# A two-layer decoder trunk on one core: modulation blocks moved out of the triangular solve into the feed-forward

## The reference, cut to what matters

```python
c_act = jax.nn.silu(c)
for l in range(DEPTH):
    mod = (c_act @ w_mod[l] + b_mod[l])[:, None, :]          # w_mod: (2, 1024, 6144)
    sh1, sc1, gt1, sh2, sc2, gt2 = jnp.split(mod, 6, axis=-1)
    h = rmsnorm(x, norm1_g[l]) * (1 + sc1) + sh1
    z = h @ w_cat                                            # one input projection
    ...                                                      # RG-LRU, differential attention, RWKV-7
    x = x + gt1 * (merged @ w_out[l])
    h2 = rmsnorm(x, norm2_g[l]) * (1 + sc2) + sh2
    x = x + gt2 * conv_gated_mlp(h2, ffn_up[l], ffn_conv_w[l], ffn_conv_b[l], ffn_down[l])
return rmsnorm(x, final_g)
```

## Time and profile before

| | |
|---|---|
| Median of 3 runs | 1259.96 us (1256.7 to 1268.15) |
| The profiled execution | 1261.44 us, of which its span 1259.6 us |
| PE busy | 1208.3 us, 96% of the span |
| DVE busy | 711.8 us, 57% |
| ACT busy | 446.4 us, 35% |
| POOL busy | 66.0 us, 5% |
| Mean granted TensorE clock | 0.989 of full speed |
| Moved from memory | 212.30 MB, 169 GB/s over the span |

### The profile page before, as it was taken

The page is one execution under the profiler, slowest core; times in us unless marked ns, Lnnn a source line. Parts: engine busy times, 40 slices in busy tenths (PEclk is TensorE's granted clock), DMA queues, the critical chain, the costliest instruction groups (busy, mean ns, idle before and its releaser), DMA issues.

```text
span 1259.6 us, 23676 instructions
## 1 busy us (share of the span) xinstructions
PE 1208.3 (96%) x10096; PEld 1098.7 (87%) x10096; DVE 711.8 (57%) x1108; ACT 446.4 (35%) x731; POOL 66.0 (5%) x108
## 2 busy tenths in 40 slices
PE   7999999989999999999999999999899999999997
PEld 6888888878788899999988788888787889999996
DVE  5465545255235689986435573525532557878643
ACT  2322234400123566664332130460012156666533
POOL 0010000011001000000000000000110200000000
PEclk8899999999999999999999999999999999999999
DMA  9755444154134456667535444333522444454530
GB/s 381 276 212 184 167 148 172 50 200 171 36 133 170 195 189 243 222 223 245 218 120 191 173 183 157 130 132 122 201 89 78 142 184 177 175 192 170 197 134 34
DMA packets 39332, 214.61 MB, mean 170 GB/s; under 512 B 6192, under 2 KB 6448, under 8 KB 19792
## 3 DMA queue, kind: packets, MB, share of 16 engines
q1 hardware_dynamic: 27728, 171.42, 37.4%
q0 software_dynamic: 11520, 41.95, 9.6%
HBM read 212.30 MB, written 1.05 MB: 169 GB/s over the span
## 4 chain that ended last, share of the span: by engine, by line
PE 90%; DMA 4%; DVE 3%; issue 1%; ACT 1%; SPq 0%; DVEq 0%; ACTq 0%
PE ps L1370 19%; PE ps L1357 12%; PE ps L1359 12%; PE ps L1358 12%; PE ps L1488 11%; PE ps L1689 7%; DMA mring<-wmod_dram 3%; PE ps L1574 3%; PE ps L1328 2%; PE ps L1335 1%; DVE macc L830 1%; PE ps L1319 1%; PE ps L1741 1%; DMA G<-wmod_dram 1%; PE ps L1565 1%
## 5 line engine op out<-in xcount | busy, mean ns | idle before, releaser
L1370 PE MATMUL ps<-H,ring 128*128 128x256 f32 x1088 | 241.7, 383 | 1.4 <-ACT H L487 1.4
L1370 PEld LDWEIGHTS ps<-H,ring 128*128 128x128 f32 x1088 | 208.1, 192 | 37.0 <-issue 9.0
L1224 DVE TENSOR_TENSOR WLO<-ring,WH 128x1024 fp32r<-128x1024 f32 x144 | 175.2, 1223 | 102.3 <-ACT WH L688 102.3
L688 ACT ACTIVATE WH<-ring 128x1024 fp32r<-128x1024 f32 x144 | 151.5, 1058 | 170.1 <-PE ps L1359 163.0
L1357 PE MATMUL ps<-HH,WH 128*128 128x256 f32 x736 | 208.3, 283 | 0.0
L1358 PE MATMUL ps<-HL,WH 128*128 128x256 f32 x736 | 208.3, 283 | 0.0
L1359 PE MATMUL ps<-HH,WLO 128*128 128x256 f32 x736 | 208.3, 283 | 0.0
L1488 PE MATMUL ps<-H,ring 128*128 128x256 f32 x768 | 179.1, 385 | 0.0
L1488 PEld LDWEIGHTS ps<-H,ring 128*128 128x128 f32 x768 | 141.7, 190 | 21.7 <-issue 1.6
L1357 PEld LDWEIGHTS ps<-HH,WH 128*128 128x128 f32 x736 | 141.3, 192 | 0.0
L1358 PEld LDWEIGHTS ps<-HL,WH 128*128 128x128 f32 x736 | 141.3, 192 | 0.0
(11 more groups left out here) (314 smaller groups left out, 1607.9 us busy)
## 6 DMA issues: line engine op xcount, KB each, us to landing
ring<-wmain_dram SPq DMA_DIRECT2D x150, 1024.0 KB, 4.8
mring<-wmod_dram POOLq DMA_DIRECT2D x80, 512.0 KB, 4.6
G<-wmod_dram SPq DMA_DIRECT2D x3, 1024.0 KB, 7.6
R<-wmod_dram SPq DMA_DIRECT2D x3, 1024.0 KB, 15.6
TK<-wmod_dram SPq DMA_DIRECT2D x2, 1024.0 KB, 21.4
C<-consts_dram SPq DMA_DIRECT2D x1, 1088.5 KB, 18.4
X<-x_t_dram SPq DMA_DIRECT2D x1, 1024.0 KB, 9.6
SW<-small_dram SPq DMA_DIRECT2D x2, 512.0 KB, 15.4
```

What stands on the lines that cost most here:

```text
L688: A(WH[:, n % 2, part], ring[:, b, part], ACT.Copy).then_inc(hi_ready, 1)
L1224: V.tensor_tensor(WLO[:, n % 2, part], ring[:, b, part], WH[:, n % 2, part].bitcast(F32), ALU.subtract).then_inc(lo_ready, 1)
L1370: last = MM(ps[:, g % 4, m * S:(m + 1) * S], w_of(g, m, i), rhs[:, i, :], start=(i == 0), stop=(i == KT - 1))
```

## The change

The solve keeps one modulation block behind each x and xt step in place of two, 8 in each layer in place of 16. So only vector 4 (10) is accumulated there, its sum takes the place in the merge where vector 5's (11's) stood, and PE's and DVE's places for a sum inside the solve are gone. Layer 0's vector 5 follows in the up stage; that pushes the later blocks back, and the down stage takes 14 blocks in place of 6: 2 in each of the first four pairs and 1 in each of the next six. Sums then stand behind down pairs 0 (vector 5), 3 (vector 6) and 10 (vector 7). Layer 1's vector 11 comes in its own down stage, which had no blocks: 1 in each of the first eight pairs, the sum behind pair 8. POOL issues layer-relative blocks up to 25 (two of them ahead) before the chunk chain and the rest after the merge's additions. DVE reads a sum one pair after PE's place for it.

```diff
-DN_BLOCKS = [1, 1, 1, 1, 1, 1, 0, 0, 0, 0, 0, 0]
-DN_SUM, DN_LAST = 1, 6
+DN_BLOCKS = [[2, 2, 2, 2, 1, 1, 1, 1, 1, 1, 0, 0], [1, 1, 1, 1, 1, 1, 1, 1, 0, 0, 0, 0]]
+DN_SUMS = [{0: 5, 3: 6, 10: 7}, {8: 11}]
...
-                mod_blocks(m0 + 18, m0 + 32)
+                mod_blocks(m0 + 18, m0 + 26)
...
-                if l == 0:
-                    mod_blocks(48, 66)
+                mod_blocks(m0 + 26, 66 if l == 0 else m0 + 32)
...
                         if par == 1 and v < 4:
-                            if (kind, v) == ("x", 2):
-                                mod_vector(6 * l + 4)
-                            mod_beside(2)
+                            mod_beside(1)
...
-                mod_vector(6 * l + 5)
+                mod_vector(6 * l + 4)
...
-                    if l == 0:
-                        if n == DN_SUM:
-                            mod_vector(6)
-                        if n == DN_LAST:
-                            mod_vector(7)
-                        mod_beside(DN_BLOCKS[n])
+                    if n - 1 in DN_SUMS[l]:
+                        mod_vector(DN_SUMS[l][n - 1])
+                    mod_beside(DN_BLOCKS[l][n])
...
-                        if (par, v) == (1, 2):
-                            pe.wait_ge(mod_ready, 6 * l + 5)
...
-                        if (kind, v) == ("x", 2):
-                            mod_sum(6 * l + 4)
...
-                mod_sum(6 * l + 5)
+                mod_sum(6 * l + 4)
...
                 for q in range(4):
                     down(0, q, True)
-                    if l == 0 and q == DN_SUM:
-                        mod_sum(6)
+                    if q in DN_SUMS[l]:
+                        mod_sum(DN_SUMS[l][q])
...
-                        if 4 + q == DN_LAST:
-                            mod_sum(7)
...
                 for q in range(4):
                     down(2, q, tail=True)
+                    if 8 + q in DN_SUMS[l]:
+                        mod_sum(DN_SUMS[l][8 + q])
                     if q >= 2:
                         ones_sum(2 * l + 2, (0, 6)[q - 2], (4, 8)[q - 2])
```

## The result

The changed kernel takes 0.9921 of the time of the kernel before, 95% interval 0.9902 to 0.994: medians of 20 runs each 1254.35 us (1248.34 to 1260.61) and 1263.95 us (1256.45 to 1271.97). That is 0.8% or 9.6 us faster; the interval leaves out 1, but the gain is under the 1% (12.6 us) that the prediction takes as the least change to be told from none.

What follows compares the result with a forecast made beforehand. PE, busy 96% of the span, was taken to bound the kernel; 1261.44 - 13.4 + 1.0 + 1.1 = 1250.1 us profiled, 1248.7 us for the median of runs, range 1245.5 to 1255.5.

Steps and rivals of the forecast that it cites:

- Part 1: Both solves: with one block per step, PE's waits for DVE's masks all go, a gain of 13.4 us.
- the 6 to 7 named as the sign: Sign for the solve: its window was to get shorter by 6 to 7 us in each layer.
- Part 2: One sum per layer moves from solve to down stage: -1.77 + 1.76 us, twice, is nothing.
- Part 3: Layer 0's down stage, two blocks per pair: PE waits 1.0 us for a transfer before vector 6's sum.
- 2T - 9.5: PE's wait in us before vector 6's sum, T being a block's landing time; nothing below T = 4.75.
- 4.9 to 7.8: Landing times in us expected in layer 0's down stage; landings outside them would show the prediction wrong.
- Part 4: Layer 0, vector 7's sum behind down pair 10: residual additions come late, PE waits 1.1 us for ACT's squares.
- Part 5: Layer 1's down stage: one block per pair in eight pairs, with the sum behind pair 8, costs nothing.
- (d): Rival, 0.04: transfers saturate in the down stage, PE waits 15.7 us at vector 6's sum; 1263.4 us, 1269 with lost clock.
- (a): Rival, 0.24: no transfer wait in the down stage, the solve gives its 13.4 us; -12.8 us, 1247.2 us.
- (b): Rival, 0.14: landings near 7.8 us move the transfer wait to the down stage, 6.1 us there; 1253.8 us.
- (c): Rival, 0.06: blocks still come late in the solve, half of the 13.4 us stays; -4.6 us, 1255.4 us.

Runs made afterwards that it cites:

- e4: The kernel before with every edit of the change made for layer 1 only, layer 0 left as it was; ratio 0.9926 to the kernel before.
- both edits: The changed kernel with vector 6's sum behind pair 4 and vector 7 read behind the residual additions; 0.9868 and, run again, 0.9862 of the kernel before.
- e6: The kernel before with 32 solve blocks read from constants already in SBUF, not transferred, so four vectors are wrong; 0.9842 of the kernel before, two runs.
- e1: The changed kernel with vector 6's sum behind down pair 4 in place of 3; 0.9875 of the kernel before.
- a0: The changed kernel again, nothing altered; 0.9906 of the kernel before, 7 runs.
- a1: The changed kernel again, nothing altered, run beside the kernel with both edits; 0.9929 of the kernel before, 12 runs.
- e2: The changed kernel with DVE reading vector 7 and forming the next norm's gain behind the residual additions of pairs 8 to 10; 0.991 of the kernel before.
- e3: The changed kernel with both edits, first time; 0.9868 of the kernel before, median 1247.02 us.
- e5: The changed kernel with unused matmuls keeping PE busy in layer 0's down stage, ahead of vector 6's sum and the squares' sum; 0.9888 of the kernel before.
- e8: The kernel with both edits run again beside the changed kernel; 0.9862 of the kernel before, median 1244.56 us.
- e7: The changed kernel with vector 6's sum behind down pair 2 in place of 3; one run, no ratio, PE waited 6.3 us before that sum.

## Why the prediction came out as it did

The forecast was 1248.7 us, 11.3 us or 0.9% less than its base; measured are 1254.35 us, 9.6 us or 0.8% less than the kernel before. Of the 5.7 us between forecast and result, 4.0 lie in the base and 1.7 in the gain. Direction and size were right. That the gain came so near was in part luck: in the profiled pair it is 5.0 us and not 11.3, because PE lost 6.3 us in layer 0's down stage that the sum doesn't have (5.2 of clock, 1.0 of wait at the first place, 0.1 at the second). The medians show 4.6 us more gain than the profiled pair, and no trace shows where, since the kernel before was profiled only once. The same holds for e4 (11.9 us by the medians, 7.3 by the stretch that it changes) and for both edits together (17.7 and 21.9 us by the medians, 14.0 and 13.1 from the first solve product on).

**Part 1** held in full. Waits for the masks in the solves went from 13.4 us to none (changed kernel), and e6 shows by itself that they were for the transfer and not for DVE's work. e4 shows layer 1's share by itself. The solve's stretch got shorter by 8.2 and 8.9 us and not by the 6 to 7 named as the sign: that sign left out the 1.8 us of the sum of part 2.

**Part 2** held: a sum costs 4.65 - 2.88 = 1.77 us in the down stage (e1), so the move is even.

**Part 3** had the right mechanism and place, and its term too small: 1.0 us against 2.0 in the first profile, 1.3, 1.6 and 3.5 in the three further runs that have the order and no filling. The formula 2T - 9.5 was 0.3 to 0.4 us low in all four, with the landings of each run put in; the rest is the landings. These were 3.9 to 6.7 us around a median of 5.2 (568 to 600) in the first profile and up to 7.9 in a0, so they left the 4.9 to 7.8 outside of which the prediction calls itself wrong; yet those that vector 6 waited for, 5.1 to 7.5 us, were inside. One landing of 7.5 us was enough for the 3.5 us of a1, and the T of the prediction was one number for all. e1 shows the cover that one pair more gives. That PE would never wait for `low` held too.

**Part 4** held: 1.2 us against 1.1, shown by e2.

**Part 5** held, shown by e4: no wait and no fallen clock.

**What failed** is that the sum has no term for the clock behind the waits of parts 3 and 4; rival (d) says of waits of about 1 us that they are shorter than those of the solve, which cost none. I had priced a fallen clock only for a wait of 15.7 us (rival d). The waits for the masks, up to 3.6 us, cost none in the two traces that have them (before and e4); waits of 1.2 to 2.0 us in the down stage of the first profile cost 1.8 and 3.4 us more. The missed term, 5.2 us, is larger than the two waits themselves, 3.2 us. So the length of a wait alone doesn't tell. Before or behind each wait of the down stage stands a sum, 1.8 us of one-column matmuls. The sum without a wait costs no clock (e1 and e3), and wait and sum together do, unless work fills the wait (e5). A sum that the change doesn't touch, in layer 0's input projection at about 90 us, says the same: in the nine profiled runs in which it follows without a wait there is no dip behind it, in the three in which PE stood 1.02, 0.53 and 0.37 us before it there is one. The shortest, in e8, and then PE's window behind it (busy, granted clock, DMA share, GB/s):

```profile
88.54 1.92 PE L1323 MATMUL ps<-sm,macc 128*128 128x1 f32 x16 [0.37 <-issue]
```

```profile
92.00:94.00 2.00, 2.00 (x6) 0.50 0.82 338
```

That is not the whole rule, though: the tail's wait and sum gave no dip in e1, and dips also follow waits without a sum (last section). What tells the cases apart is open, and a wait of the same length next to full matmuls in the down stage wasn't tried.

Of the rivals, (a), the whole gain (-12.8 us), is what both edits give, 14.0 and 13.1 us from the first solve product on; it needed an order of the down stage that the change didn't have. (b) was met halfway in a1, where the wait was 3.5 us of its 6.1. (c) and (d) did not occur.

## What to carry to other kernels

Work that hides under the busiest engine is limited by when its data come: a double buffer whose two blocks are used back to back gives the second pair no lead, the same blocks spaced out get all of it, so look at the distance between uses before you look at the length of the use. Where a step of the bounding engine needs something from a side chain, leave it a whole period of slack, and look what stands behind the reader in its engine's own order (here all the residual additions behind the read of one small vector). A short wait of TensorE next to one-column matmuls is to be priced with the clock: here waits of 1.2 to 3.5 us cost another 1.8 to 4.3 us in eight of nine places.

## What the runs showed of the hardware

The dip's price didn't grow in proportion to the wait: 3.1 to 3.4 us behind waits of 1.3, 1.6, 2.0 and 6.3 us and 4.3 us behind one of 3.5 us, with a granted clock of 0.50 to 0.53 in the first profile. Behind the wait of 1.2 us at the tail it was 1.8 us in the changed kernel, a0, a1 and e7, and nothing in e1.

Dips come without a sum as well, and not each time. In both layers of all twelve profiled runs PE waits 1.4 to 1.7 us for DVE at the end of the solve, between products of 64x64 matrices. In 22 of these 24 places the clock stayed; in e7, layer 0, and in a0, layer 1, it fell. In e7 the wait and PE's window behind it are:

```profile
304.89 1.16 PE L1635 MATMUL ps<-R,TK 64*64 64x64 f32 x64 [1.65 <-DVE R L1115]
```

```profile
307.00:313.00 6.00, 6.00 (x20) 0.50 0.00 0
```

Such dips vary from run to run at places that the change doesn't touch: in the kernel before the clock was 0.57 between 30 and 45 us, and the spread of its runs, 15 us, is wider than the whole effect of the change. A profiled run was therefore compared stretch by stretch and not by its total.
